# Twenty column pairs of the first projection as seven half-size products, with gates and conv outputs kept in DRAM and the mixer's stages in another order

## The reference: one decoder layer

```python
proj = xn @ w_in        # 1024 -> 6144: a_val, a_gate, q, k, v, g, gate_a, gate_b
u = a_val * jax.nn.sigmoid(a_gate)
conv = causal_conv31(concat(conv_buf, u)) + b_dw
a_out = silu(layer_norm(conv, conv_ln_w, conv_ln_b)) @ w_conv_out
q, k = rotary(q), rotary(k) * QK ** -0.5
S_new, o = retention_scan(q, k, v, ret_state)      # 4 heads, chunks of 128 columns
o = o * rsqrt(mean(o * o) + EPS)
b_out = (silu(g) * o) @ w_ret_out
merged = sigmoid(gate_a) * a_out + sigmoid(gate_b) * b_out
h = x + rms_norm(merged @ w_o)
y = h + rms_norm(square(relu(rms_norm(h) @ w_up)) @ w_down)
```

## Time and profile before

| | before |
|---|---|
| median of 3 runs | 1559.52 us (1559.51 to 1559.8) |
| span of the profiled execution | 1557.6 us |
| PE busy | 1527.3 us, 98% |
| DVE busy | 940.9 us, 60% |
| ACT busy | 509.5 us, 33% |
| POOL busy | 706.6 us, 45% |
| first projection and `b_out`, `a_out` (L691), share of the chain that ended last | 46% |
| FFN products (L1056), share of that chain | 38% |
| DMA | 194.87 MB, 125 GB/s on average |

### The profile page before, as it was taken

How to read it: one execution, slowest core, us unless ns; L and a number is a source line. 1 busy time by engine, 2 the same in 40 slices (tenths; PEclk the granted TensorE clock), 3 DMA queues, 4 the chain that set the end, 5 groups by cost and what they waited for, 6 DMA issues and landing times.

```text
span 1557.6 us, 27861 instructions
## 1 busy us (share of the span) xinstructions
PE 1527.3 (98%) x10926; PEld 1513.6 (97%) x10926; DVE 940.9 (60%) x1215; ACT 509.5 (33%) x710; POOL 706.6 (45%) x502
## 2 busy tenths in 40 slices
PE   6999999999999999999999999999999999999995
PEld 5999999999999999999999999999999999999995
DVE  7899959764485234411161795666656757474846
ACT  6000100242150224200111575555556433232333
POOL 1444434442244323444458345555555555455555
PEclk9999999999999999999999999999999999999998
DMA  5211121123321232111142024566667575464634
GB/s 189 92 44 48 47 62 48 41 61 100 96 102 47 75 101 81 48 48 47 47 152 87 15 76 162 191 218 244 234 231 246 208 283 210 157 218 163 218 103 163
DMA packets 99083, 194.87 MB, mean 125 GB/s; under 512 B 7968, under 2 KB 20000, under 8 KB 97072
## 3 DMA queue, kind: packets, MB, share of 16 engines
q1 hardware_dynamic: 85184, 170.48, 32.2%
q10 hardware_dynamic: 13808, 23.09, 4.5%
HBM read 137.50 MB, written 56.05 MB: 124 GB/s over the span
## 4 chain that ended last, share of the span: by engine, by line
PE 96%; DVE 2%; ACT 1%; issue 0%; POOL 0%; DMA 0%; POOLq 0%; DVEq 0%; ACTq 0%
PE ps L691 46%; PE ps L1056 38%; PE ps L982 3%; PE ps L969 3%; PE ps L807 1%; PE ps L806 1%; PE ps L810 1%; PE ps L821 1%; PE ps L791 0%; PE ps L796 0%; PE ps L888 0%; ACT xn_h L1150 0%; DVE xn_l L1717 0%; DMA x_in<-xT_dram 0%; DVE x_in L1709 0%
## 5 line engine op out<-in xcount | busy, mean ns | idle before, releaser
L607 POOL TENSOR_TENSOR w_h<-raw,zero 128x512 fp32r<-128x512 f32 x128 | 142.7, 1115 | 484.8 <-PE ps L691 376.1
L1056 PE MATMUL ps<-tx_h,w_h 128*128 128x258 f32 x960 | 271.6, 283 | 1.4 <-POOL w_l L660 0.9
L1056 PE MATMUL ps<-tx_l,w_h 128*128 128x258 f32 x960 | 271.3, 283 | 0.0
L1056 PE MATMUL ps<-tx_h,w_l 128*128 128x258 f32 x960 | 271.2, 283 | 0.0
L660 POOL TENSOR_TENSOR w_l<-raw,w_h 128x512 fp32r<-128x512 f32 x120 | 185.6, 1550 | 148.9 <-ACT w_h L1474 148.4
L691 PE MATMUL ps<-xn_h,w_h 128*128 128x344 f32 x1128 | 248.4, 326 | 2.8 <-ACT xn_h L1150 1.6
L691 PE MATMUL ps<-xn_l,w_h 128*128 128x344 f32 x1128 | 242.3, 321 | 0.0
L691 PE MATMUL ps<-xn_h,w_l 128*128 128x344 f32 x1128 | 241.3, 320 | 0.0
L1056 PE MATMUL ps<-fx_h,w_h 128*128 128x258 f32 x720 | 203.9, 283 | 0.0
L1056 PE MATMUL ps<-fx_l,w_h 128*128 128x258 f32 x720 | 203.4, 282 | 0.0
L1056 PE MATMUL ps<-fx_h,w_l 128*128 128x258 f32 x720 | 203.2, 282 | 0.0
(11 more groups left out here) (294 smaller groups left out, 2664.9 us busy)
## 6 DMA issues: line engine op xcount, KB each, us to landing
raw<-wseq_dram SPq DMA_DIRECT2D x264, 256.0 KB, 2.7
quad_scratch<-quad_h SPq DMA_DIRECT2D x16, 774.0 KB, 3.5
tx_h<-quad_scratch SPq DMA_DIRECT2D x12, 1032.0 KB, 10.0
tx_l<-hidden_scratch SPq DMA_DIRECT2D x12, 1032.0 KB, 12.1
hidden_scratch<-hq_g SPq DMA_DIRECT2D x8, 1032.0 KB, 6.9
hidden_scratch<-stg_b SPq DMA_DIRECT2D x6, 1032.0 KB, 6.9
...
```

The costliest lines, as they stand in the source:

```text
L607: pool.tensor_tensor(hi, raw[:, s, :], zero[:, 0:1].broadcast_to([P, SLOT]), ALU.add).then_inc(w_hi, 1)
L1056: out = pe.matmul(ps[:, 2 * n + s, 0:HC], RINGS[q % RING][wa][:, kk * P:(kk + 1) * P], OPS[x][xb][:, QK * kh + kk, at_:at_ + HC], start=(i ...
```

## The change

The four pairs for u stay as they were, except that the high part of their weights is now made by ACT. The other 20 column pairs (g of both head pairs, gate_a, gate_b, q, k and v) each become a unit of seven half-size products, 168 matmuls of 258 columns, as in the FFN; products 5 and 6 follow each other in the same banks as two of the earlier ones, and each product waits for the eviction of what stood in its banks.

- **Operands.** The input needs sums of its quarters: POOL forms eight (L509 to L518), ACT scales the input again and makes three high parts, DVE makes the low parts `sx_l`, all during the last three u pairs.
- **Weights.** Per unit POOL makes four sums of slots and seven low parts, eleven operations of 128 x 512; ACT makes the seven high parts. SP loads the four slots of the next unit as POOL and ACT release them.
- **Order.** The units run g, gate_a, the first gate_b, q/k/v of pair 0, three of gate_b, q/k/v of pair 1. The taps of the convolution go between the evictions of units 0 to 8 on DVE, the layer norm into units 9 to 13, the rotations of pair 0 into units 10 and 11 and those of pair 1 into units 17 and 18 (four of 258 columns in each of these units, a third and a fourth of a table at a time); the chunks of pair 0 stand in units 13 to 15 after given products (`RET_A`, `RET_B`), its norm in units 16 and 17. The chunks of pair 1 stand in the eight `a_out` slots.
- **DRAM.** The gates go to `gate_scratch`, one store of 1 MB per unit (twelve), since their place is used otherwise; the split layer-norm output goes to `conv_scratch`. After the last unit SP loads: `cva_h` and `cva_l` (8 DMAs of 516 KB), the gates `ma` (4 of 1 MB), `gt0`, `gt1` (2 MB each), and after the fourth `ro_g` the two of `gb` (2 MB each).
- **b_out.** It is multiplied as half products: six tiles take heads of pair 0 first (`product_gate` on DVE, L2521, and `product_add` on POOL), two tiles take both halves, and six take heads of pair 1; the merges follow one per slot. WO and all that follows is as before. The number of weight slots (264) and of chunks (16) is the same.

The lines that carry the argument:

```diff
+XU = 20
+OFF = 4 * XU
+G_AOUT, S_AOUT = 9, 16
+EARLY = KT - 2
...
+X_G, X_GA, X_GB, X_QKV = (0, 1, 2, 3), (4, 5, 6, 7), (8, 13, 14, 15), ((9, 10, 11, 12), (16, 17, 18, 19))
+X_RET = 13
+RET_A = {1: 0, 3: 1, 6: 2, 8: 3, 11: 4, 13: 5, 16: 6, 18: 7}
+RET_B = {2: 0, 4: 1, 7: 2, 9: 3, 12: 4, 14: 5, 17: 6, 19: 7}
...
+            last = STEPS * (XU - 1)
...
+            sp.wait_ge(xw_pm, 2 * (last + 3) + 2)
+            for j in range(CT):
+                sp.dma_start(cva_h[:, j, :].bitcast(F32), cscr[0, j]).then_inc(piece_ld[j], 16)
+            sp.wait_ge(xw_pm, 2 * (last + 4) + 2)
+            for j in range(CT):
+                sp.dma_start(cva_l[:, j, :].bitcast(F32), cscr[1, j]).then_inc(piece_ld[j], 16)
+            sp.wait_ge(xw_pm, 2 * (last + 6) + 2)
+            for s in range(2):
+                gate_stored(sp, X_GATES[-1 - s])
+            for i in range(4):
+                sp.dma_start(ma[:, 2 * i:2 * i + 2, :], gscr[KT + 2 * i:KT + 2 * i + 2].rearrange("m p n -> p m n")
+                             ).then_inc(ma_ld[i], 16)
+            sp.dma_start(gt0[:], gscr[0:4].rearrange("m p n -> p m n")).then_inc(gt_ld, 16)
+            sp.dma_start(gt1[:], gscr[4:8].rearrange("m p n -> p m n")).then_inc(gt_ld, 16)
+            std_weights(20, 24)
+            sp.wait_ge(ro_g, 4)
...
+            for v in range(XU):
+                unit_sum(v, 0)
+                unit_low(v, 0)
+                unit_low(v, 1)
+                unit_sum(v, 1)
+                unit_low(v, 2)
+                unit_sum(v, 2)
+                unit_low(v, 3)
+                unit_sum(v, 3)
+                unit_low(v, 4)
+                unit_low(v, 5)
+                unit_low(v, 6)
...
+            def unit_bank(v, i, s):
+
+                if v == 0 and i < 2:
+                    taken(pe, G_U + 6 + i)
+                elif i == 0:
+                    x_evicted(pe, v - 1, "e5")
+                elif i == 1:
+                    x_evicted(pe, v - 1, "e7")
...
+                elif i == 3:
+                    x_evicted(pe, v, "e1")
+                elif i == 4:
+                    x_evicted(pe, v, "e3")
+                elif i == 5:
+                    x_evicted(pe, v, "e4")
+                elif i == 6:
+                    x_evicted(pe, v, "e6b" if s else "e6a")
+
+            def unit_product(v, i):
+
+                q = STEPS * v + i
+                a, b, c = XBANKS[v]
+                n = (a, b, c, a, c, a, a)[i]
+                pe.wait_ge(xw_lo, q + 1)
...
+                for s in range(2):
+                    if s == 0 or i == 6:
+                        unit_bank(v, i, s)
+                    for kk in range(QK):
+                        for m, (wa, xb) in enumerate(PARTS):
+                            out = pe.matmul(ps[:, 2 * n + s, 0:HC], XRINGS[q % RING][wa][:, kk * P:(kk + 1) * P],
+                                            x_operand(i, xb, kk, s),
...
+            for v in range(XU):
+                for j in range(STEPS):
+                    unit_product(v, j)
+                    unit_turn(v, j)
+
+            CV = (cva_h, cva_l)
+            for c in range(NRC):
+                g, slot = G_AOUT + c, S_AOUT + c
...
+                        chunk_a(1, c)
+                chunk_b(1, c)
+                decode_out(1, c, 3 * (g % 2), CH + 8).then_inc(mm, 1)
...
+                unit_turn(v, 1)
+                unit_turn(v, 2)
+                unit_turn(v, 3)
+                dve.wait_ge(xw_pm, 2 * (STEPS * v + 4) + 2)
+                x_evicted(dve, v, "e4")
+                row = two(x_row(v, 2))
+                dve.tensor_tensor(row, pair(c), row, ALU.add).then_inc(xe_d, 1)
+                unit_turn(v, 4)
+                x_evicted(dve, v, "e3")
+                for s in range(2):
+                    dve.wait_ge(xw_pm, 2 * (STEPS * v + 5) + 1 + s)
+                    row = two(x_row(v, 3))[:, s, :]
+                    dve.tensor_tensor(row, ps[:, 2 * a + s, 0:HC], row, ALU.add).then_inc(xe_d, 1)
+                unit_turn(v, 5)
+                unit_turn(v, 6)
...
+                dve.wait_ge(ma_ld[c // 2], 16)
+                dve.tensor_tensor(t3(ma[:, c, :]), pset(g), t3(ma[:, c, :]), ALU.mult).then_inc(ps_free[g % 2], 1)
+                if c < 4:
+                    head_gate(0, c)
+                else:
+                    head_lo(0, c - 4)
```

1388 lines of the change are left out of this document (894 added, 494 removed).

## The result

The changed kernel takes 1587.13 us (median of 4 runs, 1586.68 to 1588.31) beside 1559.51 us for the kernel before (1559.41 to 1559.8): a ratio of 1.0176, 95% interval 1.0161 to 1.019. The forecast was 1546, its range 1524 to 1564. The profiled execution spans 1584.8 us, 27.2 more than the 1557.6 before.

A forecast was written before the change was run, and what follows sets the result against it. PE was taken as the bound, time going by its columns: 51.3 us saved, less waits and clock loss, gave -13.6. From the profiled 1557.6, plus 1.9 for the median, that made 1546 us, range 1524 to 1564.

The forecast's parts named there:

- The gain, -51.3: Twenty column pairs become units of 20.18 us in place of 22.74, saving 51.3 us of PE time.
- Start of the units, 2.6: At the first units PE waits for an eviction on DVE behind low parts and taps: 2.6 us (0 to 5).
- Gate units, 2: In units 0 to 8 and 12 to 15 evictions come late behind other DVE operations: 2 us (0 to 8).
- Rival (D): POOL's eleven operations per unit, all at 2.16 us, become the bound in the 20 units: about 1605 us; chance 0.10.
- Rotation units, 9 (2 to 16): In units 10, 11, 17 and 18 rotations on DVE, slowed by POOL, overrun the unit: 9 us (2 to 16).
- Rival (C): In the rotation units POOL and DVE never overlap, costing 26 us in four units instead of 9: 1563 us; chance 0.08.
- a_out slots 0 to 4, 15: Slots 0 and 1 wait for late gate loads, 14 us (8 to 22); gates between chunks in slots 2 to 4, 1.
- the first b_out tile, 3.5: Before b_out PE waits for the fourth tile's low part, made right after the last a_out gate: 3.5 us (3 to 6).
- the 10 us ahead of `p_b`'s product in slot 1: Sign in a_out slot 1: PE idle about 10 us before this product, released by DVE.
- WO, 3.6: At WO's eighth k-tile the last merge and low part come later than PE: 3.6 us (2 to 5).
- Clock, 2 (0 to 6): After the long wait in a_out slot 1 the PE clock falls once and matmuls run slower: 2 us (0 to 6).
- Rival (B): Clock falls after waits at unit 10, slots 0 and 1, b_out and WO, costing 10 us more: 1556 us; chance 0.12.

The follow-up runs named there:

- e3_lategate: The changed kernel with the gate products of pair 0's heads in a_out slots 2 to 5 in place of 0 to 3: 1585.04 us, ratio 1.0164.
- e10_pause: The kernel before, with PE made to wait for 14 ACT operations in a row ahead of a group of gate_a: 1574.56 us, ratio 1.0096.

## Why the prediction was wrong, point by point

**The gain, -51.3: right.** Gate units take 20.2 us, without a gap.

**Start of the units, 2.6: right in size, wrong in its place.** PE waits 2.9 us for a low part of POOL (`wx_l`), not for an eviction behind taps.

**Gate units, 2: none in units 1 to 8.** PE is busy 20.10 us of 20.10 in unit 1. In units 12 to 15, which the term covers too, PE waits 1.6 us for a sample in unit 14 and twice less than 0.5. Rival (D) is ruled out with it: POOL's operations in the units have means of 1.29 to 1.54 us, under the 1.8. (Its price was added up wrongly: 1546 + 72 - 9 is 1609, not 1605.)

**Rotation units, 9 (2 to 16): 20.3 of waiting.** The length of a rotation was sized well from the earlier trace rows: 0.774 + 0.760 + 0.692 + 0.692 + 2 x 0.611 + 2 x 0.769 = 5.68 us in the mean, where the sum had 5.5. What failed is the step after it, "two of them give part of it back", and "I put 5 on unit 10 ... and 2 each on 11 and 18". Four rotations and the evictions are 4 x 5.68 + 2.2 = 24.9 us of DVE's work, 4.7 over a unit's 20.2. The last rotations did run behind their unit's end (one of units 10 and 11 each, two of 17 and 18 each), but units 11 and 18 had as many to take over from the unit before, so that it gave them nothing back. Unit 10 in addition began its rotations 9 us late, behind the layer norm's two subtractions and 3.8 us of waiting for PE's statistics between them, and unit 11 2.9 us late, behind an eviction of ACT. The time between the units' last evictions was 28.3, 28.4, 23.1 and 27.1 us, each against 20.2. The upper end of my own term, 16, was the plain product of the numbers I had, and I went below it without a row for it.

**Rival (C) was the mechanism.** I gave it 0.08, because the mean of 0.863 seemed to speak for overlap. That mean was over operations that met POOL and others that met none: POOL was idle half of the time then. Operations that met POOL waited for its end then too, as one pair of rows of the kernel before shows:

```profile
147.51 1.04 POOL L607 TENSOR_TENSOR w_h<-raw,zero 128x512 fp32r<-128x512 f32 x1 [2.80 <-PE ps L691]
147.54 1.39 DVE L1811 TENSOR_TENSOR qk<-rtmp 64x344 f32<-64x344 f32 x1
```

My 0.87 for each operation of POOL was an average over met and unmet ones. The rival's 26 us are what the four units took above 20.2 each, 26.1, though that holds the clock and unit 10's late start too. The row of 2.16 beside low parts on DVE showed the same thing from POOL's side.

**a_out slots 0 to 4, 15, and the first b_out tile, 3.5: 17.7 of idle time, but by another wait.** The sum is near the 18.5 expected, and the trace shows the chain that I wrote down: `gt` late (T0 + 31.5 against my T0 + 25 to 27), the gate, the sample's load. The waits also lie elsewhere than I had put them: 7.8 us in slot 0, whose late start I had called hidden, 3.6 in slot 1, 3.9 in slot 4 and 2.6 ahead of b_out; the 10 us ahead of `p_b`'s product in slot 1, my sign for this term, were 2.6 and ended by ACT. `e3_lategate` shows that this chain was only the last of two: without the gate the load of `v_bc` takes 11.8 us beside the bulk, and 2.1 us are won. My sum had priced that load at its quiet 3.9 us. A wait that ends last in a trace is not yet the wait whose removal pays.

**WO, 3.6: 3.1 measured.**

**Small waits that the sum had not, 6.4:** what is left of the 50.4; among them 3.0 for `osq`, the squares of the heads' norm, 1.6 for a sample in unit 14 and 1.0 for `bop`.

**Clock, 2 (0 to 6): 24.2, and 28.1 with what is not located.** This is the term that turned the sign. I counted one fall, behind the longest wait; there were twelve. Rival (B) had the mechanism and under half of its price: "four or five restarts at 2 us each". `e10_pause` measured 1.9 us for one, and the twelve come to 2.0 each, so the price was right; what was wrong is the number of times. The clock does come back to 1.00 between them. The Trainium skill ("TensorE: Matmul & The Clock Gate", section "HAM oscillation — how this bites in real kernels") describes a kernel that pays anew in every round of a loop because each has a wait; the a_out stage, with a fall of its own behind the waits that end at 623.2, 640.0, 676.6 and 714.1, agrees with it.

In sum: waiting 50.4 where I had 35.7 without the clock, and 28.1 lost inside the busy time where I had 2. Rivals (B) and (C) came together. I had priced each by itself beside a forecast without them, although both hang on the same thing: if the rotations wait, the clock falls. A range made from rivals that are taken one at a time leaves out just the case that happened; and even both at my prices, 1546 + 10 + 17 = 1573, stay 14 us under the result, because the falls of the clock were counted too few.
